# Six plain chunks instead of eight ahead of the seven-product pairs, and token-side sums made in two sets of banks

## The chip, the cores and the metric

The kernel runs on one NeuronCore of a Trainium2 chip. The metric is the device time of one execution in microseconds (us), as the median of several runs. The engines are TensorE (PE, matrix products), VectorE (DVE), ScalarE (ACT), GpSimd (POOL) and SyncE (SP, which issues the loads of weights). Each takes its instructions in order, and semaphores are the only coupling between them.

## The reference, cut to what matters

Two transformer blocks on a sequence of 512 tokens of width 1024, in float32. Each ends in a feed-forward with a hidden width of 4096, which is the part that is changed:

```python
h = rms_norm(x, norm2_g[l])
f = jnp.square(jax.nn.relu(jnp.einsum('bsd,df->bsf', h, w_ff1[l])))
x = x + jnp.einsum('bsf,fd->bsd', f, w_ff2[l])
...
h = rmsnorm(x, g_pre_mlp[layer])
u = jax.nn.relu(jnp.einsum('bsd,df->bsf', h, w_up[layer]))
y = jnp.einsum('bsf,fd->bsd', u * u, w_down[layer])
```

## The kernel before

Float32 accuracy is had from three products of rounded parts: each operand is split into a high part (`xh`, `wh`, `uh`) and a low rest (`xl`, `wl`, `ul`), and `three` issues high by high, high by low and low by high. Weights come as a stream of "chunks" of 128x1024 through four slots (chunk n in slot n % 4). SP loads `raw`, POOL rounds it to `wh` and subtracts for `wl`, and `split_ready` counts the chunks split.

Each feed-forward is done in two halves of 16 hidden tiles: an up run that makes 16 tiles of `uh` and `ul`, then a down run of 16 chunks that reads them. There are two feed-forwards, so four up runs (0 to 3). An up tile is made in one of two ways:

- A plain chunk: 24 matmuls of 512 columns (all tokens). The first three plain chunks of a run are interleaved (`several`), the others follow alone (`chunk_transposed`). PE writes chunk c to bank c % 4; the tile is evacuated with a relu, squared by ACT, and its rest is taken by DVE (`rest_of_tile`, called `rest(c)`).
- A pair: two chunks by the two halves of the tokens (EARLY, LATE), as a 2x2 product with seven products instead of eight. Each product is 12 matmuls of 256 columns. Products 1, 2 and 6 use `xh` and `xl`; products 3, 4, 5 and 7 use token-side sums (`t_high`, `t_low`), which are made once per feed-forward; products 3 to 6 use weight-side sums, which DVE makes in banks 6 and 7 for each pair (`weight_sums_first`, `weight_sums_last`), ACT rounds (`sum_round`) and DVE subtracts from (`weight_rest`). DVE also adds the seven products together (`first_corner` to `fourth_product`).

Runs 0 and 2 (the first of each feed-forward) have 8 plain chunks (`PLAIN`) and 4 pairs; runs 1 and 3 have 8 pairs. The plain chunks keep PE at work while the token-side sums are made. These come in four steps k, one for each two of the eight tiles of x: ACT writes two scaled parts (`scaled_parts`), DVE forms four sums of 256 columns over them (`t_sums` part 0), ACT rounds them (`t_round`), and DVE takes the rests (`t_sums` part 1, counted by `t_ready`). All steps use banks 4 and 5, so that step k+1 can't begin before step k is finished.

The norm's sum of squares (`norm_sums`, four transposes of `ss` into bank 7) stands in PE's queue behind the first three matmuls of plain chunk 5; `norm_total` of DVE reduces bank 7.

The order on each engine is the order of the code. For DVE it is `plain_run` and `pair_run`, for ACT `plain_tiles` and `pair_tiles`, for PE `feed_first`, `pair` and `feed_forward`, for POOL `split_rounds`, `split_chunk` and `split_pairs`.

Of the kernel before, what the change touches and what calls it, by code (L numbers as in the profile page):

```python
# [27 lines left out]
F32 = mybir.dt.float32  # L28
# [4 lines left out]
P = 128  # L33
# [30 lines left out]
PLAIN = 8  # L64
# [97 lines left out]
for _name, _n in (("norm1", 8), ("norm2", 8), ("final", 8), ("pre_mix", 8), ("post_mix", 8),  # L162
# [11 lines left out]
             (C_FF2 + 2 * FH, 3 * FH, FH // 2))  # L174
ROW_ORDER = ((0, 1, 2, 3), (1, 2, 3, 0))
# [28 lines left out]
def slot_of(p, role):  # L204

    return (PAIR_RUNS[run_of(p)][0] + role) % SLOTS
# [12 lines left out]
def build(nc, a):  # L219
    ctx = ExitStack()  # L220
    with ctx:
# [13 lines left out]
        def sem(name):  # L235
# [90 lines left out]
        t_high = [at(f"t_high{i}", [P, 4, Q], F32R, o) for i, o in  # L326
                  enumerate((behind, behind + 8192, tmb_at, tmp_at))]
        t_low = [at(f"t_low{i}", [P, 4, Q], F32R, o + 4096) for i, o in
                 enumerate((behind, behind + 8192, tmb_at, tmp_at))]
# [25 lines left out]
        x4_bank = [bank[4], bank[5], bank[6]]  # L355

# [77 lines left out]
        def product_bank(p, i):  # L434
            return bank[(7 * place_in(p) + i + run_of(p) // 3) % 5][:, EARLY]
# [109 lines left out]
        def _(pool):  # L545
# [137 lines left out]
            def split_pair(p):  # L683
# [41 lines left out]
            split_rounds(C_FF1 // SLOTS, (C_FF1 + PLAIN) // SLOTS)  # L725
            split_pairs(0)
# [11 lines left out]
            second_round = (C_FF2 + 3) // SLOTS  # L738
            for n in range(second_round * SLOTS, second_round * SLOTS + SLOTS):
                split_chunk(n)  # L740
                if n == C_FF2 + 3:
                    x4_squares()

            for n in range(second_round * SLOTS + SLOTS, C_FF2 + PLAIN):
                split_chunk(n)
# [15 lines left out]
        def _(pe):  # L761
# [334 lines left out]

            def feed_first(c0, e0, xl0, i, squares, between=None):
# [19 lines left out]
            def pair(p):  # L1117
# [8 lines left out]
                if alone:  # L1126
                    pe.wait_ge(evacuated, e - 3)
# [6 lines left out]
                if alone:  # L1134
                    pe.wait_ge(evacuated, e - 2)
# [8 lines left out]
                if alone and run in (0, 2):  # L1144
                    pe.wait_ge(t_ready, 32 if run else 16)
# [334 lines left out]
        def _(act):  # L1480
# [179 lines left out]
            def scaled_parts(k, gain):  # L1660

                if k:
                    act.wait_ge(t_ready, 4 * k - 2)
                A(bank[4][:, EARLY], x[:, k % 4, EARLY], ACT.Copy, scale=col(gain, k % 4)).then_inc(scaled_part, 1)
                act.wait_ge(t_ready, 4 * k)
                A(bank[5][:, EARLY], x[:, 4 + k % 4, LATE], ACT.Copy, scale=col(gain, 4 + k % 4)
                  ).then_inc(scaled_part, 1)

            def t_round(k):

                act.wait_ge(t_made, 4 * k + 4)
                for t, src in enumerate((bank[4][:, EARLY], bank[4][:, LATE], bank[5][:, EARLY], bank[5][:, LATE])):
                    A(t_high[t][:, k % 4], src, ACT.Copy).then_inc(t_rounded, 1)

            def sum_round(p, i):
# [3 lines left out]
                if place_in(p) == 0:  # L1679
                    act.wait_ge(chunk_done, chunk_of(p) - 3 + role)  # L1680
# [26 lines left out]
            def plain_tiles(c0, first, norm, k0, p, gain):  # L1707

                for c in range(PLAIN):
                    if c < 4:  # L1710
                        t_round(k0 + c)
# [7 lines left out]
                    if c < 3:  # L1719
                        scaled_parts(k0 + c + 1, gain)  # L1720
                    if c == PLAIN - 3:
                        norm_sd(norm)
                        sum_round(p, 0)
                        sum_round(p, 1)
                    if c == PLAIN - 2:
                        sum_round(p, 2)
                        sum_round(p, 3)
# [16 lines left out]
            act.wait_ge(xl_ready, KT + 6)  # L1744
            scaled_parts(0, "norm2")
# [204 lines left out]
            scaled_parts(4, "pre_mlp")  # L1950
# [1061 lines left out]
```

## Time and profile before

| | |
|---|---|
| median of 3 runs | 1085.52 us (1083.82 to 1086.12) |
| the profiled execution | 1085.29 us, of which the span from first to last instruction is 1083.6 us |
| PE busy | 1066.3 us, 98% of the span |
| DVE, POOL, ACT busy | 703.4, 672.5, 400.6 us |
| mean granted PE clock | 0.998 |

Busy shares are averages over the whole span. In the two changed stretches (about 158 to 230 us and 766 to 834 us) the engines have other shares: in 163.3 to 185.5 us DVE is busy for 20.08 of 22.20 us. A row of the timeline gives the start, the duration, the engine and the line, then what is written and read, and in brackets the engine's idle time ahead of it.

### The profile page before, as it was taken

To read this page: it belongs to the slowest core of one execution; us is meant where nothing else is said; L and a number is where in the kernel's file an instruction comes from. 1 tells how busy PE (TensorE), PEld (TensorE's weight loads), DVE (VectorE), ACT (ScalarE), POOL (GpSimd) and SP (SyncE) were. 2 spreads that over 40 slices of the span, in tenths; PEclk is the share of its full clock that TensorE was granted. 3 is DMA by queue.
4 is the path that set the end of the run, shared out by engine and by line. 5 is a ranking of instruction groups with operands and counts; after the bars stand their busy time and mean duration, and the time that the engine had idled before them with its cause. 6 is when DMAs were issued, how large, how long until landed. Compare 5 with 4: busy or idle time off the path is not lost.

```text
span 1083.6 us, 17261 instructions
## 1 busy us (share of the span) xinstructions
PE 1066.3 (98%) x6163; PEld 933.5 (86%) x6163; DVE 703.4 (65%) x1381; ACT 400.6 (37%) x817; POOL 672.5 (62%) x460
## 2 busy tenths in 40 slices
PE   9999999999999999999999999999999999999997
PEld 6878888998899988888788787677899888999886
DVE  5999778951158853447689878676888113886033
ACT  5156565540015541220211346655765000465012
POOL 7979856577645586667566333135856764557762
PEclk9999999999999999999999999999999999999999
DMA  7421223243223343334443232112123931234412
GB/s 261 137 96 60 69 88 98 87 147 117 97 65 111 117 156 103 110 97 138 128 123 97 79 90 67 40 53 85 59 97 124 204 102 61 96 118 168 182 59 77
DMA packets 52251, 115.54 MB, mean 107 GB/s; under 512 B 21840, under 2 KB 22480, under 8 KB 52176
## 3 DMA queue, kind: packets, MB, share of 16 engines
q1 hardware_dynamic: 31200, 105.40, 29.4%
q10 hardware_dynamic: 20976, 9.15, 3.4%
q8 instruction: 46, 0.75, 0.3%
q14 instruction: 29, 0.24, 0.1%
HBM read 105.09 MB, written 4.19 MB: 101 GB/s over the span
## 4 chain that ended last, share of the span: by engine, by line
PE 73%; DVE 18%; ACT 3%; issue 2%; POOL 2%; ACTq 1%; DMA 0%; SPq 0%; DVEq 0%; POOLq 0%
PE bank L766 71%; DVE bank L2118 5%; DVE work L2620 2%; DVE max L2613 2%; ACTq L1780 1%; DVE tmp L2010 1%; PE bank L1296 1%; POOL wl L567 1%; DVE work L2598 1%; DVE ropey L2568 1%; ACT wh L1683 1%; DMA x<-xT 0%; DVE wl L2377 0%; DVE ropey L2574 0%; DVE bank L2010 0%
## 5 line engine op out<-in xcount | busy, mean ns | idle before, releaser
L567 POOL TENSOR_TENSOR wl<-raw,wh 128x1024 fp32r<-128x1024 f32 x140 | 333.7, 2384 | 11.7
L564 POOL TENSOR_SCALAR wh<-raw 128x1024 fp32r<-128x1024 f32 x139 | 148.9, 1071 | 236.1 <-PE bank L766 181.6
L766 PE MATMUL bank<-xh,wh 128*128 128x512 f32 (+2 forms) x747 | 257.5, 345 | 2.7 <-ACT vg L1577 1.5
L766 PE MATMUL bank<-xh,wl 128*128 128x512 f32 (+2 forms) x747 | 249.1, 337 | 0.0
L766 PE MATMUL bank<-xl,wh 128*128 128x512 f32 (+2 forms) x744 | 246.9, 339 | 0.2 <-DVE xl L2029 0.2
L766 PEld LDWEIGHTS bank<-xh,wh 128*128 128x128 f32 x747 | 142.4, 191 | 33.6 <-issue 19.5
L766 PEld LDWEIGHTS bank<-xl,wh 128*128 128x128 f32 x744 | 141.4, 191 | 13.7 <-DVE xl L2029 3.1
L766 PEld LDWEIGHTS bank<-xh,wl 128*128 128x128 f32 x747 | 142.6, 191 | 11.3
L1683 ACT ACTIVATE wh<-bank 128x512 fp32r<-128x512 f32 x96 | 52.2, 596 | 241.8 <-DVE bank L2362 103.1
L766 PE MATMUL bank<-uh,wh 128*128 128x512 f32 x320 | 123.2, 385 | 1.8 <-DVE ss L2412 0.9
L766 PE MATMUL bank<-uh,wl 128*128 128x512 f32 x320 | 121.3, 379 | 0.0
L766 PE MATMUL bank<-ul,wh 128*128 128x512 f32 x320 | 117.4, 379 | 0.0
L766 PE MATMUL bank<-t_high,wh 128*128 128x256 f32 x384 | 107.1, 279 | 0.3 <-DVE sq L2418 0.2
L766 PE MATMUL bank<-t_high,wl 128*128 128x256 f32 x384 | 105.6, 275 | 0.0
L766 PE MATMUL bank<-t_low,wh 128*128 128x256 f32 x384 | 105.6, 275 | 0.0
L766 PE MATMUL bank<-wh,uh 128*128 128x512 f32 x256 | 97.1, 379 | 0.4 <-POOL wl L567 0.4
L766 PE MATMUL bank<-wh,ul 128*128 128x512 f32 x256 | 97.1, 379 | 0.0
L766 PE MATMUL bank<-wl,uh 128*128 128x512 f32 x256 | 97.0, 379 | 0.0
L2377 DVE TENSOR_TENSOR wl<-bank,wh 128x512 fp32r<-128x512 f32 x96 | 63.3, 683 | 24.3 <-ACT wh L1683 24.0
L2010 DVE TENSOR_TENSOR bank<-bank,rb 128x512 f32<-128x512 f32 x16 | 11.2, 699 | 100.8 <-PE bank L766 100.8
L701 POOL TENSOR_SCALAR wh<-raw 128x512 fp32r<-128x512 f32 x24 | 14.9, 620 | 98.9 <-PE bank L766 98.9
L766 PEld LDWEIGHTS bank<-t_high,wh 128*128 128x128 f32 x384 | 73.6, 192 | 1.6 <-issue 0.6
(338 smaller groups left out, 2108.0 us busy)
## 6 DMA issues: line engine op xcount, KB each, us to landing
raw<-wstream SPq DMA_DIRECT2D x188, 512.0 KB, 3.5
x<-xT SPq DMA_DIRECT2D x8, 256.0 KB, 4.6
x4rows<-x_rows ACTq DMA_DIRECT2D x4, 512.0 KB, 7.2
out<-x4rows SPq DMA_DIRECT2D x8, 256.0 KB, 2.1
qd<-ropey ACTq DMA_DIRECT2D x16, 64.0 KB, 2.1
kd<-ropey ACTq DMA_DIRECT2D x16, 64.0 KB, 2.4
qa<-ropey SPq DMA_DIRECT2D x16, 64.0 KB, 2.1
ka<-ropey SPq DMA_DIRECT2D x16, 64.0 KB, 2.0
```

The lines of the kernel that those rows point to most:

```text
L564: nc.gpsimd.tensor_scalar(wh[c][:], raw[c][:], 1.0, 1.0, ALU.mult, ALU.mult).then_inc(high_ready, 1)
L567: nc.gpsimd.tensor_tensor(wl[c][:], raw[c][:], wh[c][:].bitcast(F32), ALU.subtract).then_inc(split_ready, 1)
L701: nc.gpsimd.tensor_scalar(high_b[:, 0:512], b[:, 512:], 1.0, 1.0, ALU.mult, ALU.mult).then_inc(high_ready, 1)
L766: return nc.tensor.matmul(out, stationary, moved, start=start, stop=stop)
L1296: last = nc.tensor.transpose(out[:, j * P:j * P + P], probs[2 * (n % 3) + e][:, j * P:j * P + P], ident[:])
L1683: A(wh[slot_of(p, role)][:, 512 * part:512 * part + 512], bank[7 - made % 2][:], ACT.Copy).then_inc(sum_rounded, 1)
L1780: act.dma_start(dst[p0:p0 + 32, 2 * m + hh // 2, cs], ropey[32 * hh:32 * hh + 32, g % 2, part, cs]).then_inc(rope_moved[g % 2], 16)
L2010: return V.tensor_tensor(out, p, q, ALU.mult)
L2118: ins = V.scalar_tensor_tensor(out=out, in0=src, scalar=w, in1=acc, op0=ALU.mult, op1=ALU.add)
L2377: V.tensor_tensor(wl[slot][:, at], bank[7 - made % 2][:], wh[slot][:, at].bitcast(F32), ALU.subtract).then_inc(sum_ready, 1)
L2613: V.max(max8[:, q], work[:, q + 1, 0:N]).then_inc(top_step, 1)
L2620: V.match_replace(work[:, q + 1, 0:N], max8[:, q], work[:, q + 1, 0:N], TAKEN).then_inc(top_step, 1)
```

## The change

`PLAIN` goes from 8 to 6, so runs 0 and 2 have 6 plain chunks and 5 pairs. With fewer plain chunks the rest of the stage is rearranged:

- The token-side sums of steps 1 and 3 use banks 6 and 7 (`t_banks`), those of 0 and 2 banks 4 and 5. High and low parts of all four sums lie in two tensors `t_sides`, so that ACT rounds a whole bank (512 columns) in one instruction and DVE takes the rest of a whole bank in one: two instead of four each per step.
- Bank 7 is also where the norm's squares are transposed to. So PE waits in `feed_norm`, ahead of the norm's transposes, until all four steps are finished (`t_ready` 8 or 16).
- ACT waits for all eight low parts of x and for the sum of squares before the first scaled parts, since banks 6 and 7 are in use until then.
- The four slots shift by two: the weight sums of the first pair go to slots 0 to 3 as the last plain chunks leave them (`free_at`). Product 1 of the first pair goes to bank 3 and product 2 to bank 4 (`FIRST_BANK`).
- DVE and ACT have a new written order. ACT now does the tile of the last plain chunk ahead of the rounding of the first pair's weight sums.
- Four operations of a few elements each (`row_scale` to `row_weight_mean`) move from the front of `pair_run(2)` to behind it.

```diff
-PLAIN = 8
+PLAIN = 6
+FIRST_BANK = (3, 0, 3, 1)
 def slot_of(p, role):
-    return (PAIR_RUNS[run_of(p)][0] + role) % SLOTS
+    first, _, count = PAIR_RUNS[run_of(p)]
+    return (first + 2 * count + role) % SLOTS
+def free_at(p, role):
+    first = PAIR_RUNS[run_of(p)][0]
+    return first - SLOTS + (slot_of(p, role) - first) % SLOTS + 1
...
+        t_banks = [(bank[4], bank[5]), (bank[6], bank[7])]
...
+            def feed_norm(i, squares):
+                pe.wait_ge(t_ready, 16 if i == 13 else 8)
+                norm_sums(i, ss, 0, sq_added, squares)
...
-                    hooks = {0: lambda: norm_sums(i, ss, 0, sq_added, squares)} if c == 5 else {}
+                    hooks = {0: lambda: feed_norm(i, squares)} if c == PLAIN - 1 else {}
...
             def t_round(k):
                 act.wait_ge(t_made, 4 * k + 4)
-                for t, src in enumerate((bank[4][:, EARLY], bank[4][:, LATE], bank[5][:, EARLY], bank[5][:, LATE])):
-                    A(t_high[t][:, k % 4], src, ACT.Copy).then_inc(t_rounded, 1)
+                for sides, b in zip(t_sides, t_banks[k % 2]):
+                    A(sides[:, :, 0, k % 4], two(b[:]), ACT.Copy).then_inc(t_rounded, 1)
...
             def sum_round(p, i):
-                    act.wait_ge(chunk_done, chunk_of(p) - 3 + role)
+                    act.wait_ge(chunk_done, free_at(p, role))
...
-            act.wait_ge(xl_ready, KT + 6)
-            scaled_parts(0, "norm2")
+            act.wait_ge(xl_ready, 2 * KT)
+            act.wait_ge(sq_added, 2 * KT)
...
-                t_rest(0, t1, 2)
-                t_rest(1, t2, 2)
-                t_rest(2, t3, 4)
-                t_rest(3, t4, 4)
+                t_rest(0)
+                t_rest(1)
```

DVE, the beginning of run 0: behind the norm's last sum (written to `ss`) and up to the second plain tile. `L2326`/`L2345` are the sums of part 0, `L2331`/`L2351` the rests of part 1, `L2436`/`L2456` the evacuation of a tile, `L2422`/`L2440` its rest. Before:

```order
L2326 SCALAR_TENSOR_TENSOR bank4<-x_49,cols_72,bank4 128x256 [waits scaled_part]
...
L2326 SCALAR_TENSOR_TENSOR bank5<-x_49,cols_72,bank4 128x256 [waits t_made]
L2436 TENSOR_SCALAR sq0_75<-bank0 128x512 [waits chunk_done,sq_added]
L2331 TENSOR_TENSOR t_low0_143<-bank4,t_high0_139 128x256 [waits t_rounded]
...
L2331 TENSOR_TENSOR t_low3_146<-bank5,t_high3_142 128x256 [waits t_rounded]
L2422 TENSOR_TENSOR ul_65<-sq0_75,uh_64 128x512 [waits square_ready]
```

and in the changed kernel:

```order
L2345 SCALAR_TENSOR_TENSOR bank4<-x_49,cols_72,bank4 128x256 [waits scaled_part]
...
L2345 SCALAR_TENSOR_TENSOR bank6<-x_49,cols_72,bank6 128x256 [waits scaled_part]
...
L2345 SCALAR_TENSOR_TENSOR bank7<-x_49,cols_72,bank6 128x256 [waits t_made]
L2351 TENSOR_TENSOR t_sides0_139<-bank4,t_sides0_139 128x2x256 [waits t_rounded]
L2351 TENSOR_TENSOR t_sides1_140<-bank5,t_sides1_140 128x2x256 [waits t_rounded]
L2456 TENSOR_SCALAR sq0_75<-bank0 128x512 [waits chunk_done,sq_added]
L2351 TENSOR_TENSOR t_sides0_139<-bank6,t_sides0_139 128x2x256 [waits t_rounded]
L2351 TENSOR_TENSOR t_sides1_140<-bank7,t_sides1_140 128x2x256 [waits t_rounded]
```

The sums of the second step now stand ahead of the rests of the first, and up to the last rest there are three evacuations and two rests of tiles between them.

PE, plain chunk 5 of run 0, in bank 1 (`ident` by `ss` into bank 7 are the norm's transposes). Before:

```order
L766 MATMUL bank1<-xh_50,wh1_57 128x512 [waits evacuated,split_ready]
L766 MATMUL bank1<-xl_51,wh1_57 128x512
L766 MATMUL bank1<-xh_50,wl1_61 128x512
L867 MATMUL bank7<-ident_66,ss_74 128x128 [waits sq_added,bc_used]
L867 MATMUL bank7<-ident_66,ss_74 128x128 x3
```

and in the changed kernel:

```order
L772 MATMUL bank1<-xh_50,wh1_57 128x512 [waits evacuated,split_ready]
L772 MATMUL bank1<-xl_51,wh1_57 128x512
L772 MATMUL bank1<-xh_50,wl1_61 128x512
L873 MATMUL bank7<-ident_66,ss_74 128x128 [waits sq_added,bc_used,t_ready]
L873 MATMUL bank7<-ident_66,ss_74 128x128 x3
```

The place in the queue is the same, with one more wait; behind it stand the other 21 matmuls of the chunk, which is now the last plain one.

ACT, the end of the plain tiles of run 0 (`L1715`/`L1723` the relu of a tile, `L1717`, `L1718`/`L1725`, `L1726` its squares, `L1683`/`L1693` the rounding of weight sums, `L1691`/`L1701` the copy of the first product). Before:

```order
L1683 ACTIVATE wh1_57<-bank7 128x512 [waits chunk_done,sum_made]
L1683 ACTIVATE wh1_57<-bank6 128x512 [waits chunk_done,sum_made]
L1715 ACTIVATE sq0_75<-bank2 128x512 [waits ul_ready,chunk_done]
L1717 ACTIVATE uh_64<-sq0_75 128x512 [waits evacuated]
L1718 ACTIVATE sq0_75<-sq0_75 128x512
L1683 ACTIVATE wh2_58<-bank7 128x512 [waits chunk_done,sum_made]
```

and in the changed kernel:

```order
L1723 ACTIVATE sq1_76<-bank1 128x512 [waits ul_ready,chunk_done]
L1725 ACTIVATE uh_64<-sq1_76 128x512 [waits evacuated]
L1726 ACTIVATE sq1_76<-sq1_76 128x512
L1693 ACTIVATE wh1_57<-bank7 128x512 [waits chunk_done,sum_made]
L1693 ACTIVATE wh1_57<-bank6 128x512 [waits chunk_done,sum_made]
L1693 ACTIVATE wh2_58<-bank7 128x512 [waits chunk_done,sum_made]
```

The tile of bank 1 is that of the last plain chunk; it now stands ahead of all four roundings.

## Rows read from the trace of the kernel before

**Rows 1.** The page, part 1: busy time, share of the span, instructions.
```profile
span 1083.6 us, 17261 instructions
...
PE   1066.3 (98%) x6163; PEld 933.5 (86%) x6163; DVE 703.4 (65%) x1381; ACT 400.6 (37%) x817; POOL 672.5 (62%) x460
```
**Rows 2.** Waits of PE's matmuls: total us, times, longest.
```profile
PE bank L766 <- DVE soft L2671: 1.6, 1, 1.6
```
**Rows 3.** Timeline of PE, first feed-forward: start, us, instruction.
```profile
177.52 0.60 PE L867 MATMUL bank<-ident,ss 128*128 128x128 f32 x4
...
192.85 0.27 PE L766 MATMUL bank<-xh,wh 128*128 128x256 f32 x1
...
230.37 0.38 PE L766 MATMUL bank<-uh,wh 128*128 128x512 f32 x1
...
313.69 0.27 PE L766 MATMUL bank<-xh,wh 128*128 128x256 f32 x1
...
323.07 0.28 PE L766 MATMUL bank<-xh,wh 128*128 128x256 f32 x1
```
**Rows 4.** Timeline of DVE, first feed-forward.
```profile
162.72 0.68 DVE L2309 TENSOR_TENSOR ss<-sq,bank 128x512 f32<-128x512 f32 x1
...
168.28 2.22 DVE L2422 TENSOR_TENSOR ul<-sq,uh 128x512 fp32r<-128x512 f32 x1
170.43 1.78 DVE L2326 SCALAR_TENSOR_TENSOR bank<-x,cols,bank 128x256 f32<-128x256 f32 x4
172.12 0.68 DVE L2436 TENSOR_SCALAR sq<-bank 128x512 f32<-128x512 f32 x1
172.94 1.42 DVE L2331 TENSOR_TENSOR t_low<-bank,t_high 128x256 fp32r<-128x256 f32 x4
...
190.72 1.29 DVE L2377 TENSOR_TENSOR wl<-bank,wh 128x512 fp32r<-128x512 f32 x2
```
**Rows 5.** Timeline of ACT, first feed-forward.
```profile
161.92 0.46 ACT L1666 ACTIVATE bank<-x,cols 128x256 f32<-128x256 f32 x1
...
185.52 0.62 ACT L1715 ACTIVATE sq<-bank 128x512 f32<-128x512 f32 x1
...
187.22 0.58 ACT L1715 ACTIVATE sq<-bank 128x512 f32<-128x512 f32 x1
...
190.02 1.09 ACT L1683 ACTIVATE wh<-bank 128x512 fp32r<-128x512 f32 x2 [0.84 <-DVE bank L2362]
```
**Rows 6.** Timeline of POOL beside the 2.22 us row of DVE.
```profile
167.57 2.38 POOL L567 TENSOR_TENSOR wl<-raw,wh 128x1024 fp32r<-128x1024 f32 x1
169.92 1.49 POOL L564 TENSOR_SCALAR wh<-raw 128x1024 fp32r<-128x1024 f32 x1
```
**Rows 7.** Timeline of DVE, second feed-forward.
```profile
769.42 1.80 DVE L2326 SCALAR_TENSOR_TENSOR bank<-x,cols,bank 128x256 f32<-128x256 f32 x4 [2.38 <-ACT bank L1666]
...
802.95 0.42 DVE L2385 TENSOR_TENSOR sq<-bank,first_product 128x256 f32<-128x256 f32 x1
...
812.33 0.42 DVE L2385 TENSOR_TENSOR ss<-bank,first_product 128x256 f32<-128x256 f32 x1
...
822.10 0.41 DVE L2385 TENSOR_TENSOR sq<-bank,first_product 128x256 f32<-128x256 f32 x1
```
**Rows 8.** Timeline of PE, second feed-forward.
```profile
779.94 0.60 PE L867 MATMUL bank<-ident,ss 128*128 128x128 f32 x4
...
795.27 0.27 PE L766 MATMUL bank<-xh,wh 128*128 128x256 f32 x1
...
834.16 0.40 PE L766 MATMUL bank<-wh,uh 128*128 128x512 f32 x1
```
**Rows 9.** Timeline of PE behind its longest wait; busy times of 600.5 to 604 us.
```profile
599.24 1.25 PE L766 MATMUL bank<-kd,qd 64*128 64x384 f32 x4 [1.60 <-DVE soft L2671]
600.42 0.74 PE L766 MATMUL bank<-xh,wh 128*128 128x512 f32 x1
...
600.50:604.00 3.50, 3.50 (x9) 2.79 (x10) 3.46 (x9) 0.00 (x0) 0.82 (x1) 0.51 0.37 125
```

More of the change, by code:

```diff
@@ L325, in build @@
                        for r in range(len(PAIR_RUNS))]
[L326 to L329, printed above, removed]
+        t_sides = [at("t_sides0", [P, 2, 2, 4, Q], F32R, behind), at("t_sides1", [P, 2, 2, 4, Q], F32R, tmp_at)]
+        t_high = [t_sides[i // 2][:, i % 2, 0] for i in range(4)]
+        t_low = [t_sides[i // 2][:, i % 2, 1] for i in range(4)]
         work = at("work", [P, TB, S], F32, behind)
@@ L434, in product_bank @@
         def product_bank(p, i):
-            return bank[(7 * place_in(p) + i + run_of(p) // 3) % 5][:, EARLY]
+            return bank[(7 * place_in(p) + i + FIRST_BANK[run_of(p)]) % 5][:, EARLY]
         def col(name, k, n=1):
@@ L725, in _ @@
             split_rounds(C_FF1 // SLOTS, (C_FF1 + PLAIN) // SLOTS)
+            for n in range((C_FF1 + PLAIN) // SLOTS * SLOTS, C_FF1 + PLAIN):
+                split_chunk(n)
             split_pairs(0)
@@ L736, in _ @@
             split_rounds(last_round + 1, (C_FF2 + 3) // SLOTS)
-            second_round = (C_FF2 + 3) // SLOTS
-            for n in range(second_round * SLOTS, second_round * SLOTS + SLOTS):
+            for n in range((C_FF2 + 3) // SLOTS * SLOTS, C_FF2 + PLAIN):
                 split_chunk(n)
@@ L1134, in pair @@
                 if alone:
-                    pe.wait_ge(evacuated, e - 2)
+                    if run in (0, 2):
+                        pe.wait_ge(t_ready, 14 if run else 6)
                     if run == 3:
@@ L1144, in pair @@
                 if alone and run in (0, 2):
-                    pe.wait_ge(t_ready, 32 if run else 16)
+                    pe.wait_ge(t_ready, 16 if run else 8)
                 pe.wait_ge(sum_ready, 4 * p + 1)
@@ L1707, in plain_tiles, with squared @@
             def plain_tiles(c0, first, norm, k0, p, gain):
-                for c in range(PLAIN):
-                    if c < 4:
-                        t_round(k0 + c)
+                def squared(c):
                     if c >= 4:
@@ L1718, in plain_tiles @@
                     A(sq[c % 2][:], sq[c % 2][:], ACT.Square).then_inc(square_ready, 1)
[L1719 to L1727, printed above, removed]
+                scaled_parts(k0, gain)
+                scaled_parts(k0 + 1, gain)
+                t_round(k0)
+                t_round(k0 + 1)
+                scaled_parts(k0 + 2, gain)
+                squared(0)
+                scaled_parts(k0 + 3, gain)
+                t_round(k0 + 2)
+                squared(1)
+                t_round(k0 + 3)
+                squared(2)
+                squared(3)
+                squared(4)
+                norm_sd(norm)
+                squared(5)
+                sum_round(p, 0)
+                sum_round(p, 1)
+                sum_round(p, 2)
+                sum_round(p, 3)
             def pair_tiles(run):
@@ L2327, in scaled_less, with t_rest @@
                                            ).then_inc(t_made, 1)
-                def t_rest(t, src, rounded):
-                    dve.wait_ge(t_rounded, 4 * k + rounded)
-                    V.tensor_tensor(t_low[t][:, k % 4], src, t_high[t][:, k % 4].bitcast(F32), ALU.subtract
-                                    ).then_inc(t_ready, 1)
+                def t_rest(i):
+                    dve.wait_ge(t_rounded, 2 * k + i + 1)
+                    sides = t_sides[i]
+                    V.tensor_tensor(sides[:, :, 1, k % 4], two(t_banks[k % 2][i][:]),
+                                    sides[:, :, 0, k % 4].bitcast(F32), ALU.subtract).then_inc(t_ready, 1)
                 if part == 0:
```

58 lines of the change are left out of this document (31 added, 27 removed).

## The prediction

> **What bounds the kernel now.** I read the page first, then the waits of PE, then the timelines of PE, DVE, ACT and POOL over the two changed stretches. PE is busy for 1066.3 of 1083.6 us [rows 1], and its longest wait for another engine in the whole span is 1.6 us [rows 2]: whatever is taken from PE's own stream is gained, and whatever it is made to wait for is lost. The other engines matter only where one of them is late for PE.
>
> What a plain chunk and a pair cost PE is read from starts. From 230.37 to 313.69 us PE does 16 plain chunks of the down run and four transposes (about 0.4 us): 82.9 / 16 = 5.18 us a chunk [rows 3]. From 313.69 to 323.07 it does one pair: 9.38 us, or 1.34 us a product [rows 3]. Run 0's four pairs take 230.37 - 192.85 = 37.52 us, exactly four times 9.38: PE never waits there. Run 2's four take 834.16 - 795.27 = 38.89 us [rows 8], 1.37 us more. The reason is DVE: it starts `first_corner` of successive pairs at 802.95, 812.33 and 822.10 us, so up to 9.77 us apart [rows 7], which is longer than PE's 9.38, and at the first of them it is 802.95 - (795.27 + 2.68) = 5.0 us behind the product that it adds. So a lag of some 5 us is all that PE can hide, and beyond that a pair costs 9.77 instead of 9.38 us.
>
> **The matmuls.** Twice, two plain chunks (10.36 us) become one pair (9.38 us): -0.98 us each, **-1.96** in all. Had nothing else to be paid, 1083.3 us would follow.
>
> **The wait ahead of the norm's transposes.** PE comes to them at 177.52 us in run 0 [rows 3], and nothing ahead of that place in its queue is changed. Before, they waited for squares that were long there; now they wait for all rests of the token-side sums, and 21 matmuls of the chunk and every pair are queued behind them. When is DVE done? The norm's last sum ends at 162.72 + 0.68 = 163.40 us [rows 4]. ACT now begins only then, and two scaled parts at some 0.4 us apart, the second 0.46 long [rows 5], bring DVE's first sum to 164.4. From there DVE has, up to the last rest:
>
> - 4 steps of four sums, each step 172.12 - 170.43 = 1.69 us [rows 4]: 6.76.
> - 8 rests of 512 columns in two rows of 256. No such row exists. Four rests of 256 columns take 1.42 us, 0.36 each [rows 4]: the bounds are one of them (0.36, twice the columns at no more time) and two (0.71, nothing saved). `L2377` has 512 columns and reads a bank and a rounded tensor in the same way: two in 1.29, which is 0.61 start to start beside the tail [rows 4]. I take that, the same kind and size: 4.88 (2.9 to 5.7 by the bounds).
> - 3 evacuations of 0.68, 0.60 start to start: 1.80 [rows 4].
> - 2 rests of tiles, 0.61 each undisturbed: 1.22.
>
> That is 14.66 us, and 0.1 for the last one's end: 179.15 us with no idle time at all. Before, this same work had until 192.85 + 2.68 = 195.5 us (product 3). Idle time comes on top. A rest of a tile can stretch: the row at 168.28 lasted 2.22 us because it stood still until POOL's `L567` ended at 167.57 + 2.38 = 169.95, and POOL's next, at 169.92, was held in turn (1.49 us) [rows 4, 6]. Each of the two rests can so cost 0 to 1.6 us. I take 0.85 for both and for the waits on ACT: 180.0 us, a wait of **2.5 us** in run 0 (bounds 1.6 and 4.9, or 0.5 with rests of 0.36).
>
> The Trainium skill, SBUF — State Buffer, section "SBUF: two separate sides", has the rule behind the stretched row: DVE and GpSimd share a pair of ports under an exclusive lock, which a VectorE operation with two SBUF inputs needs and whoever comes first keeps for the whole instruction. By that rule the new rests, which read a bank, are never held; if they were, as the two tile rests are, eight holds of up to 1.6 us would come on top. The stretched and held rows agree with it, and `L2377` rows show no stretch.
>
> In run 2 the sums start at 769.42 us [rows 7] and PE comes at 779.94 [rows 8]: only 10.5 us for the same 14.76, which gives 784.2. With 0.3 of idle time, 784.5: a wait of **4.6 us** (bounds 4.2 and 7.4, or 2.6 with rests of 0.36). A part of it falls earlier, since the evacuation of chunk 0 now stands behind four steps' worth of DVE work and chunk 4 needs its bank.
>
> **The first pair.** Its weight sums go into slot 1, which the last plain chunk holds, and ACT does that chunk's tile first. From the end of the chunk (its last matmul's result is there some 0.15 us after PE moves on): relu and two squares 187.22 - 185.52 = 1.70 [rows 5], rounding 0.60 (two in 1.09), DVE's rest 0.68 [rows 4], and 0.15 for three handovers: 3.3 us. Product 3 needs it after 2.68: a wait of 0.6. Then DVE has two weight sums, a tile rest, a reciprocal and another rest, ACT a rounding between, again about 3.2 to 3.3 us from the first rest to the third, which product 5 needs 2.68 us behind product 3: 0.5. With a matmul's slow restart after each wait, **1.2 us** (bounds 0.6, and 2.8 if that tile rest is held by POOL once).
>
> **The following pairs.** DVE then starts `first_corner` some 5 us behind PE, just the lag that run 2 had at its start [rows 7]. What followed there is what follows now in both runs, with one pair more: the pairs from the third on cost 9.77 instead of 9.38, **0.9 us** in each run (bounds 0.4 and 1.6). In run 2 the 1.37 us that were lost before are replaced by these: -1.37. The four small operations moved behind run 2 free DVE of about 1.8 us ahead of `first_corner`, and the lag above is reckoned without them.
>
> **The sum at full clock.** Run 0: -0.98 + 2.5 + 1.2 + 0.9 = +3.6. Run 2: -0.98 + 4.6 + 1.2 + 0.9 - 1.37 = +4.35. Together +8.0 us. Runs 1 and 3, both down runs and the attention are not touched; PE is as full there as before and gives nothing back.
>
> **PE's clock.** Behind its 1.60 us wait and four small matmuls the granted clock of 600.5 to 604.0 us is 0.51, so the lower level of 1.2 GHz, and nine matmuls take that stretch, where the chunks above (5.18 / 24 = 0.216 us a matmul) would have 16 in it [rows 9]: about 1.6 us lost. PE's new waits, 2.5 and 4.6 us, are longer than that, so a fall behind the second is likely and behind the first an even chance. A fall costs 1.6 us, but DVE goes on meanwhile and its lag shrinks, so that about 0.5 comes back: +1.1 each. One fall is the likeliest: **+9.1 us** on 1085.29, 1094.4. The profiled execution lies 0.23 us below the median of the runs shown, so this is 1094.6 for the median; I round towards the case without a fall and say **1094.2**.
>
> The Trainium skill, TensorE: Matmul & The Clock Gate, section "Why this matters for your kernels", advises against idle gaps between bursts of matmuls because TensorE's clock falls back to half. By it the second wait here, the longest of the kernel, is at risk and the first less so; without any such fall the sum would be the +8.0 above.
>
> **Rivals.**
> - *The sums are in time* (the other side). If DVE reached its last rest by 177.5 and 780 us, only -1.96 and up to -1.37 of run 2's old loss would remain: 1082.2 to 1083.6. It needs DVE to do 14.66 us of back-to-back work in 13.1 and 10.5 us; the point from which it decides is a rest of 512 columns at under 0.41 us for run 0 and under 0.1 us for run 2, so only run 0 could get there, and run 2 would then still wait 2.6 with rests of 0.36. For it speaks only that the rests' shape is new. Chance 0.05.
> - *Only the norm's wait is real*: ACT's order and DVE's lag are hidden. Then -1.96 + 2.5 + 4.6 - 1.37 = +3.8, 1089.3. For it: run 0 had no loss in its pairs before. Against: its DVE lag at the start was smaller, and the chain from the last chunk to product 3 is longer than 2.68 us by rows. Chance 0.08.
> - *The clock never falls*: +8.0, 1093.5. Against it stands only one row, that of 1.60 us; chance 0.27.
> - *One fall or two* (forecast): +9.1 to +10.2, 1094.6 to 1095.7. Chance 0.48.
> - *Worse*: POOL holds the tile rests ahead of both waits and in the first pairs, +3 more: 1097 to 1099. Each hold exists in rows; several together are rare. Chance 0.10.
> - *The wait moves PE into DVE's time and the two cancel*, no change within 0.2% (about what a measurement of this kernel can tell from none): 0.02.
>
> **How the numbers follow.** Faster 0.05, same 0.02, slower 0.93. The range reaches from between the second rival and the sum at full clock to the beginning of the worst case: 1090.5 to 1097.0 leaves out about 2 in 10.
>
> **What the changed profile should show.** A wait of PE for DVE ahead of the transposes of `ss` (`L873`), 2 to 3 us near 180 and 4 to 5 us near 784; DVE without idle time in the 15 us ahead of each; `t_sides` rests of about 0.61 us start to start; two waits of about half a microsecond at the third and fifth product of the first pair, for DVE's `wl`; five pairs in 48.5 to 49.5 us instead of 46.9; a stretch with a granted clock near 0.5 behind the second wait. The prediction is wrong if the transposes start at 177.5, or if the pairs of run 0 take 46.9 us.

## The result and the profile after

The changed kernel takes 1097.04 us in the median of four executions (1095.14, 1095.27, 1098.81, 1102.96), the kernel before 1084.67 (1083.72 to 1086.12); the ratio is 1.0124, with a 95% interval of 1.0107 to 1.0141. The sign and the mechanisms are as forecast, but the median lies above the range that ended at 1097.0. The execution in the trace is the fastest one, 1095.14 us (forecast for it: 1094.4). Most of what a longer execution has more lies outside the feed-forwards; run e1 shows it.

The page of the changed kernel, part 1 (answers to [rows 1]), and then those waits of PE's matmuls that are new or stood at the top before (total, times, longest; answers to [rows 2]):

```profile
span 1093.4 us, 17399 instructions
...
PE   1066.1 (98%) x6235; PEld 933.9 (85%) x6235; DVE 710.7 (65%) x1395; ACT 405.2 (37%) x811; POOL 667.3 (61%) x462
```
```profile
PE bank L873 <- DVE t_sides L2351: 6.1, 2, 3.7
PE bank L772 <- issue: 1.7, 3, 0.9
PE bank L772 <- DVE wl L2395: 1.7, 2, 1.3
PE bank L772 <- DVE tmp L2082: 1.5, 1, 1.5
PE bank L772 <- DVE soft L2697: 1.5, 1, 1.5
```

PE is busy as long as before and the span is 9.8 us longer: the loss is in waits. The first and the third row are new, and so is most of the second. Their places are in the timeline of PE (start, duration, and in brackets the idle time ahead):

```profile
180.74 0.66 PE L873 MATMUL bank<-ident,ss 128*128 128x128 f32 x4 [2.35 <-DVE t_sides L2351]
...
185.77 0.27 PE L772 MATMUL bank<-xh,wh 128*128 128x256 f32 x1
...
196.56 0.28 PE L772 MATMUL bank<-xh,wh 128*128 128x256 f32 x1
...
224.71 0.28 PE L772 MATMUL bank<-xh,wh 128*128 128x256 f32 x1
...
234.48 0.38 PE L772 MATMUL bank<-uh,wh 128*128 128x512 f32 x1
...
777.69 0.45 PE L772 MATMUL bank<-xh,wh 128*128 128x512 f32 x1 [0.57 <-DVE sq L2456]
...
787.47 1.11 PE L873 MATMUL bank<-ident,ss 128*128 128x128 f32 x4 [3.71 <-DVE t_sides L2351]
...
794.08 0.27 PE L772 MATMUL bank<-xh,wh 128*128 128x256 f32 x1
...
797.79 0.46 PE L772 MATMUL bank<-t_sides,wh 128*128 128x256 f32 x2 [0.87 <-issue]
...
806.11 0.28 PE L772 MATMUL bank<-xh,wh 128*128 128x256 f32 x1
...
834.26 0.29 PE L772 MATMUL bank<-xh,wh 128*128 128x256 f32 x1
...
844.04 0.38 PE L772 MATMUL bank<-wh,uh 128*128 128x512 f32 x1
```

Both waits for the token-side sums stand ahead of the transposes, and chunk 4 of run 2 waits too (777.69), as the forecast said. The first pairs take 196.56 - 185.77 = 10.79 and 806.11 - 794.08 = 12.03 us instead of 9.38, the next three in either run (224.71 - 196.56) / 3 = 9.38, the last ones 9.77 and 9.78.

DVE ahead of and in the first pair of run 2, and POOL beside it:

```profile
797.00 1.29 DVE L2395 TENSOR_TENSOR wl<-bank,wh 128x512 fp32r<-128x512 f32 x2 [5.76 <-ACT wh L1693]
...
799.53 1.74 DVE L2440 TENSOR_TENSOR ul<-sq,uh 128x512 fp32r<-128x512 f32 x1
```
```profile
799.45 1.27 POOL L705 TENSOR_TENSOR wl<-raw,wh 128x512 fp32r<-128x512 f32 x1
```

DVE idles 5.76 us there: for the first three the slot is still held by the last plain chunk, which PE ends at 794.08, and then ACT does that chunk's tile (1.7 us) ahead of the rounding. And a tile's rest stands still until POOL's operation ends at 800.72. That hold is most of why run 2's first pair costs 1.2 us more than run 0's: the rest takes 1.74 us, the same one in run 0 takes 0.86.

The granted clock (the eighth value) of 4 us behind either wait, and of 3.5 us at the place of [rows 9]:

```profile
180.70:184.70 4.00, 3.96 (x21) 3.53 (x22) 3.96 (x5) 1.64 (x4) 1.14 (x1) 1.00 0.01 4
787.50:791.50 4.00, 4.00 (x14) 3.44 (x15) 3.69 (x6) 2.83 (x6) 0.00 (x0) 0.60 0.00 0
```
```profile
604.60:608.10 3.50, 3.50 (x18) 2.58 (x17) 3.50 (x7) 0.33 (x3) 1.33 (x1) 1.00 0.28 68
```

Of the two waits only the second is followed by the lower level of the clock. Behind the wait of 1.5 us near 604 it stays up here, though the kernel before fell there. By the starts of its matmuls the changed kernel gets 1.7 us back at this place (from 600.42 to 604.80 it took 4.38 us, from 604.95 to 607.64 it takes 2.69). Some 0.4 of it had been lost ahead, at a wait of 0.17 us in the attention, so that the stretch between the feed-forwards is 1.3 us shorter in all.

### The profile page after: what moved, and what is told of

Read it like the earlier page. It is cut to its first block, busy times and chain, and to the rows that moved or that the text cites. A ratio compares the mean times of both kernels' runs of the same rounds, so it can differ in the third digit from the quotient of the medians.

```text
span 1093.4 us, 17399 instructions
## 1 busy us (share of the span) xinstructions
PE 1066.1 (98%) x6235; PEld 933.9 (85%) x6235; DVE 710.7 (65%) x1395; ACT 405.2 (37%) x811; POOL 667.3 (61%) x462
## 4 chain that ended last, share of the span: by engine, by line
PE 70%; DVE 20%; issue 3%; ACT 3%; POOL 2%; ACTq 1%; DMA 1%; SPq 0%; DVEq 0%; POOLq 0%
PE bank L772 69%; DVE bank L2136 5%; DVE work L2646 2%; DVE max L2639 2%; ACTq L1799 1%; DVE bank L2345 1%; DVE tmp L2028 1%; PE bank L1308 1%; DVE t_sides L2351 1%; POOL wl L575 1%; DVE bank L2028 1%; DVE work L2624 1%; DVE xl L2047 1%; DMA x<-xT 1%; DVE ul L2440 0%
## 5 line engine op out<-in xcount | busy, mean ns | idle before, releaser
L575 POOL TENSOR_TENSOR wl<-raw,wh 128x1024 fp32r<-128x1024 f32 x136 | 323.8, 2381 | 11.3
L572 POOL TENSOR_SCALAR wh<-raw 128x1024 fp32r<-128x1024 f32 x135 | 144.0, 1067 | 235.1 <-PE bank L772 178.2
L772 PE MATMUL bank<-xh,wh 128*128 128x512 f32 (+2 forms) x739 | 251.8, 341 | 3.0 <-ACT vg L1589 1.5
L772 PE MATMUL bank<-xh,wl 128*128 128x512 f32 (+2 forms) x739 | 243.2, 333 | 0.0
L772 PE MATMUL bank<-xl,wh 128*128 128x512 f32 (+2 forms) x736 | 241.0, 335 | 1.1 <-DVE xl L2047 1.0
L1693 ACT ACTIVATE wh<-bank 128x512 fp32r<-128x512 f32 x104 | 56.5, 595 | 249.4 <-DVE bank L2380 100.5
L772 PE MATMUL bank<-t_sides,wh 128*128 128x256 f32 x832 | 144.7, 277 | 3.1 <-DVE wl L2395 1.7
L772 PEld LDWEIGHTS bank<-t_sides,wh 128*128 128x128 f32 x832 | 126.1, 192 | 5.0 <-DVE wl L2395 2.1
L772 PE MATMUL bank<-t_sides,wl 128*128 128x256 f32 x416 | 114.4, 275 | 0.0
L2395 DVE TENSOR_TENSOR wl<-bank,wh 128x512 fp32r<-128x512 f32 x104 | 68.5, 682 | 33.1 <-ACT wh L1693 33.1
L772 PEld LDWEIGHTS bank<-t_sides,wl 128*128 128x128 f32 x416 | 79.9, 192 | 0.0
```

What stands on the lines that cost most here:

```text
L572: nc.gpsimd.tensor_scalar(wh[c][:], raw[c][:], 1.0, 1.0, ALU.mult, ALU.mult).then_inc(high_ready, 1)
L575: nc.gpsimd.tensor_tensor(wl[c][:], raw[c][:], wh[c][:].bitcast(F32), ALU.subtract).then_inc(split_ready, 1)
L772: return nc.tensor.matmul(out, stationary, moved, start=start, stop=stop)
L1693: A(wh[slot_of(p, role)][:, 512 * part:512 * part + 512], bank[7 - made % 2][:], ACT.Copy).then_inc(sum_rounded, 1)
L2395: V.tensor_tensor(wl[slot][:, at], bank[7 - made % 2][:], wh[slot][:, at].bitcast(F32), ALU.subtract).then_inc(sum_ready, 1)
```

## The experiments

Each is timed beside the kernel before on the same chip; its median there was 1083.97 to 1084.3 us. "Undisturbed" means the executions of a kernel's lowest level (in e2 and e11 a single one). e2 to e4, e6, e7, e9 to e14 are edits of the changed kernel, e5 and e8 of the kernel before.

**e1: the changed kernel again.**

> The changed kernel once more, to see how its executions spread. The one in the trace took 1095.14 us, others 1095.27, 1098.81 and 1102.96 at a mean clock of 0.997, 0.996 and 0.993. Theory 'spread by the new waits': the times again lie between 1095 and 1103 while those of the kernel before stay within 3 us of each other; the longer ones have a lower mean clock; a profile over 1096 us shows a stretch near half clock at a place where the trace of 1095.14 us has full clock, behind one of the new waits (run 0's transposes or the first pairs). Rival 'spread of the chip': the kernel before spreads as widely in the same rounds, or all executions of the changed one lie within 1094.5 to 1096.

Six executions: 1096.54, 1096.66, 1103.7, 1104.61, 1104.83, 1105.1; those of the kernel before, eleven, lie within 1083.54 to 1086.82. The execution in the trace is that of 1105.1. PE's longest wait in 500 to 580 us (the only other one there is 0.6), and the matmul that waited:

```profile
PE bank L772 <- DVE tmb L2028: 5.4, 1, 5.4
```
```profile
564.64 0.80 PE L772 MATMUL bank<-wh,xh 128*128 128x512 f32 x1 [5.36 <-DVE tmb L2028]
```

That is in the attention, at the index scores, 330 us behind the changed code. Followed back from there: DVE in this stage is held by POOL time and again (the row at 551.58 lasts 2.60 us, in the first trace 0.48).

```profile
551.58 2.60 DVE L2621 TENSOR_SCALAR work<-sq,wnat 128x512 f32<-128x512 f32 x1
...
557.42 3.80 DVE L2624 SCALAR_TENSOR_TENSOR work<-sq,wnat,work 128x512 f32<-128x512 f32 x2 [0.68 <-ACT sq L1819]
```
```profile
551.20 2.69 POOL L575 TENSOR_TENSOR wl<-raw,wh 128x1024 fp32r<-128x1024 f32 x1
...
558.02 2.67 POOL L575 TENSOR_TENSOR wl<-raw,wh 128x1024 fp32r<-128x1024 f32 x1
```

The first of these holds, two rows of DVE and the two of POOL beside them:

```profile
527.49 1.34 DVE L2624 SCALAR_TENSOR_TENSOR work<-tmp,wnat,work 128x256 f32<-128x256 f32 x1
528.87 2.35 DVE L2629 TENSOR_TENSOR work<-work,mask 128x128 f32<-128x128 f32 x1
```
```profile
527.52 1.04 POOL L572 TENSOR_SCALAR wh<-raw 128x1024 fp32r<-128x1024 f32 x1 [2.90 <-PE bank L772]
528.64 2.42 POOL L575 TENSOR_TENSOR wl<-raw,wh 128x1024 fp32r<-128x1024 f32 x1
```

In the first trace the row of 1.34 us lasts 0.49 (525.51) and is nearly over when POOL starts (525.96), and the one behind it lasts 1.11. DVE meets POOL here because it is 0.4 us late from 525 us on, and it is late because ACT is. ACT issues eight rope transfers (`qd<-ropey`) ahead of its copies of the scores. This group in the kernel before, and here:

```profile
513.43 5.01 ACTq L1780 DMA_DIRECT2D qd<-ropey  x8
```
```profile
519.16 6.04 ACTq L1799 DMA_DIRECT2D qd<-ropey  x8
```

Seven issues last at most 0.61 us and one, at 522.91, lasts 1.65. In 523.0 to 523.2 us the DMA view names a packet of another kind:

```profile
q8 instruction: 1, 0.02, 35.4%
```

So a transfer of 16 KB of instructions passes just there. In the trace of the kernel before such packets stand in 501.2 to 501.3, 524.7 to 524.8 and 553.8 to 553.9 us. Only the first meets issues, those of the group ahead (one of which is 1.26 us long), and no wait of PE follows. In the changed kernel's first trace they stand in 521.5 to 521.6 and 547.7 to 547.8. PE itself is 4.1 us later there (234.48 against 230.37), so in its program they have moved forward by 7 and 10 us: it has 72 matmuls more in the two feed-forwards, half of them ahead of this place, and so more instructions. That execution, of 1095.14 us, had a lengthened issue too (eight in 5.61 us) and came through with a wait of 0.2. The clock falls behind the wait of 5.4 us (0.50 in 564.6 to 568.6 us) and behind the transposes at 180 us (0.57), which it didn't in the first trace. Of the 9.9 us between the two traces 6.9 arise between the two feed-forwards, 1.7 are the fall of the clock at 180 us, and 1.4 a longer fall behind the second wait (803.99 - 795.97 = 8.02 us from the transposes to the first pair, 6.61 in the first trace). Theory "spread by the new waits" has this one part right, the clock.

**e2: the norm's transposes later.** In `feed_first`:

```diff
-hooks = {0: lambda: feed_norm(i, squares)} if c == PLAIN - 1 else {}
+hooks = {6: lambda: feed_norm(i, squares)} if c == PLAIN - 1 else {}
```

> The norm's wait and transposes stand behind 21 matmuls of the last plain chunk instead of 3 (in both feed-forwards). Theory 'place': the waits of 2.5 and 3.7 us and the clock's fall of 1.6 us are paid because 21 matmuls stand behind them; they go and nothing comes for them: about 1087.5 us against 1095.1. Rival 'backlog of DVE': norm_total, and with it weight_sums_first in the same bank 7, now comes later on DVE, and the wait reappears at product 3 of the first pair for wl, some 2 to 3 us longer than it was there; only the clock's fall is saved: 1093 to 1094 us.

Undisturbed 1093.97 us (median 1099.49, ratio 1.0125, 1.0104 to 1.0146). No wait for `t_sides` is left, but one at product 3 of each first pair:

```profile
189.66 0.76 PE L772 MATMUL bank<-t_sides,wh 128*128 128x256 f32 x2 [3.79 <-issue]
```

It was 0.52 there. "Backlog of DVE" is right: 2.35 us are removed, and 3.3 us come back. Behind both waits the clock falls. The execution in the trace (1098.97 us) has a wait of 3.1 us at the index scores too.

**e3: ACT rounds first.** In `plain_tiles`, `squared(5)` stands behind `sum_round(p, 1)`:

```diff
-squared(5)
 sum_round(p, 0)
 sum_round(p, 1)
+squared(5)
```

> ACT rounds the first pair's two first weight sums ahead of the tile of the last plain chunk (relu and two squares, 1.7 us), in both feed-forwards; nothing else is changed. Theory 'order on ACT': the first pair's excess (1.4 us in run 0, 2.65 in run 2 over 9.38) is ACT's tile in front of the rounding; it goes, and 1091 to 1091.5 us result. Rival 'DVE is full anyway': the pairs' work is DVE's 9.77 us a pair, so later pairs take 9.77 instead of 9.38 and give most of it back: 1093.5 to 1094.5 us. Both waits ahead of the transposes stay at 2.5 and 3.7 us.

Undisturbed 1092.86 us (median 1094.45, ratio 1.0099, 1.0077 to 1.0121). No wait is left in the first pairs, but the five pairs take 48.43 us in either run instead of 48.71 and 49.96: all of them cost 9.45 to 9.8, none 9.38. "DVE is full anyway" is the nearer theory; only where POOL's hold was avoided, in run 2, 1.5 us are gained.

**e4: both edits.**

> The norm's transposes behind 21 matmuls, and ACT's two roundings ahead of the last plain tile, together. Theory 'backlog of DVE': in the former alone the wait at product 3 was 3.95 us, of which ACT's tile of 1.7 us is a part, so 1.4 to 1.7 us of each go: 1090.5 to 1091.5 us for the undisturbed executions (1093.97 and 1092.86 for either alone). Rival 'sum of both': -1.2 and -2.3 add up, 1091.6. Rival 'nothing more': 1092.5 or above.

Executions of 1088.7, 1088.82, 1090.93, 1090.99, 1094.1 and 1094.2 us; median 1090.96, ratio 1.0064 (1.0047 to 1.0081). The lowest level is some 2 us below all three expectations: with the waits cut to 1.5 and 1.2 us in run 0 and 1.9 and 0.6 in run 2, PE's clock doesn't fall in either feed-forward (mean 0.998).

**e6: matmuls in the wait.** In `feed_norm`, whose results in bank 4 nothing uses:

```diff
+pe.wait_ge(t_ready, 14 if i == 13 else 6)
+for k in range(WARM):  # 12
+    mm(bank[4][:], wh[...][:, 0:P], xh[:, k % 8], start=True, stop=True)
 pe.wait_ge(t_ready, 16 if i == 13 else 8)
```

> Twelve extra matmuls of 512 columns (their result in bank 4 is not used) run between t_ready 6 (14) and t_ready 8 (16), that is inside the norm's wait, 2.6 us of work at 0.216 us each. Theory 'clock': the waits for DVE stay, but the granted clock behind the second one stays at 1.0, the 1.6 us of it are saved (less what DVE's lag takes back), 1093.5 to 1094.5 us in the median, and the executions of 1098 and 1103 us are gone. Rival 'no effect': t_ready 6 comes too late or the matmuls delay the transposes by some of their 2.6 us: 1095 us or more.

Undisturbed 1093.23 us, 1.9 below 1095.14; median 1094.53, ratio 1.0099 (1.0079 to 1.0118). The clock behind both waits is 1.00: 1.6 us of the second wait's cost is the clock. The executions of 1099 us remain; the one in the trace has the attention's 5.4 us.

**e5: the kernel before, with the small operations moved behind `pair_run(2)`** (the last hunk of the change alone).

> The kernel before, with nothing but the four small operations of the row scale moved behind run 2's pairs. Theory 'DVE's lag': they take about 1.8 us ahead of first_corner; DVE starts the pairs that much earlier and the 1.37 us that run 2 lost shrink to 0 to 0.4: 1082.7 to 1083.2 us against 1084.0. Rival 'no effect': POOL and ACT set those holds, 1083.8 to 1084.2.

Median 1083.24 us (1082.68 to 1084.98), ratio 0.9990 (0.9982 to 0.9999). Run 2's pairs take 833.38 - 795.47 = 37.91 us instead of 38.89: 0.98 of the 1.37 us are back. "DVE's lag" is right.

**e7, e8: where the instructions' transfers fall.** Waits that have long been met, spread over PE's products of run 1 (`PADS` places with the pair of waits below; the expectations count one extra instruction for each):

```diff
 for k in range(4):
+    if done[0] < PADS and run_of(pairs[0]) == 1 and k in (1, 2, 3):
+        pe.wait_ge(split_ready, 1)
+        pe.wait_ge(split_ready, 2)
+        done[0] += 1
```

> The changed kernel with 60 extra waits on semaphores that have long been reached, spread over PE's products of run 1, so that the 16 KB instruction transfers of queue q8 come about 6 us earlier in the attention's stage (near 515 and 541.5 us instead of 521.6 and 547.8) and meet none of ACT's rope transfers. Theory 'instruction transfers': ACT's issues last 0.61 us each there, PE's wait of 5.4 us near 556 us and the half clock behind it are gone in every execution: all times within 1094 to 1098 us, median 1095.5 (a fall of the clock behind the wait at 180 us may still add 1.6). Rival 'chance of the ports': the spread has nothing to do with these transfers, and half of the executions or more stay at 1103 to 1105, median near 1100.

> The kernel before with 76 such waits in the same products, so that its instruction transfers stand to the attention's stage as they do in the changed kernel (near 517.5 and 543.6 us instead of 524.8 and 553.9); its feed-forwards are not touched. Theory 'instruction transfers': it gets the wait near 552 us in a part of its executions, with 1090 to 1093 us there and 1084 to 1085 in the others, median above 1085. Rival: 1083.5 to 1087 as ever, median 1084.

e7 missed its aim: the packet came in 520.3 to 520.4 us, still beside the issues (519.2 to 525.4), and the executions are spread as before, 1094.66 to 1104.97 (median 1099.18); it tells nothing of executions that are free of the packet. e8 met its: the packet stands in 517.8 to 517.9 us, eight issues last 6.43 us, one of them 2.03, and PE waits at the index scores:

```profile
514.00 6.43 ACTq L1788 DMA_DIRECT2D qd<-ropey  x8
```
```profile
559.47 0.80 PE L767 MATMUL bank<-wh,xh 128*128 128x512 f32 x1 [5.36 <-DVE tmb L2018]
```

Four of twelve executions take 1090.78 to 1091.41 us, the others 1084.33 to 1086.3; the median is 1085.08 (ratio 1.0016, 1.0000 to 1.0033). Of the unpadded kernel before none of the 64 timed beside these runs took more than 1086.82. The feed-forwards are untouched in it.

**e9, e13: the changed kernel with 112 such waits.**

> The changed kernel with 112 instead of 60 extra waits. With 60, the transfer of queue q8 stood at 520.39 us, still inside ACT's issues of 519.2 to 525.4, so that run tested nothing; 52 more should move it by 2.5 to 5 us, ahead of the first of them. Theory 'instruction transfers': the two groups of issues last 5.0 us each, no wait of 5.4 us near 556 to 560 us in any execution, times within 1094 to 1098, median 1096. Rival: executions of 1102 to 1105 remain although no transfer meets an issue.

> The kernel with 112 extra waits once more, since it had only four executions (1094.03 to 1096.22). Theory 'instruction transfers': again none above 1098. Rival 'chance': with the rate of the unpadded kernel (about half of the executions at 1102 to 1105) some six more executions hold about three of them.

In e9 the packets stand in 511.3 to 511.4 and 535.5 to 535.6 us. The first meets the group ahead and one issue there lasts 1.65 us, without harm; the group in question is free, and so is the next:

```profile
516.95 5.01 ACTq L1807 DMA_DIRECT2D qd<-ropey  x8
```

All eight executions lie within 1094.03 and 1096.45 us, medians 1094.86 and 1095.11, ratios 1.0098 (1.0083 to 1.0112) and 1.0098 (1.0082 to 1.0113). Without the waits six of ten had lain at 1098.8 or above.

**e14: e4 with the 112 waits.**

> The late transposes and early roundings with the 112 waits. Without them the executions were 1088.7, 1088.8, 1090.9, 1091.0, 1094.1 and 1094.2. Theory 'instruction transfers': only 1088 to 1091 remain (the rest is TensorE's clock), median 1089.5. Rival 'chance': the level of 1094 stays.

Five executions within 1087.99 and 1089.75 us, median 1088.26, ratio 1.0039 (1.0025 to 1.0052): both upper levels of e4 are gone.

Over all sixteen traces the picture is this. In six of them (before, e5, e9, e12, e13, e14) no packet meets the first group of eight `qd` issues, the group lasts 5.0 to 5.2 us, and PE doesn't wait at the index scores. In the other ten a packet meets it. Where it then lasts 6.04 us or more (e1, e6, e7, e8), PE waits 5.4 us. Where it lasts 5.54 to 5.99, the wait is 0.2 to 0.5 us, but 3.1 in e2 (5.95).

**e11, e10: short rests.** In the second feed-forward the eight rests of the sums have 64 instead of 512 columns, and its products read `t_high` in place of `t_low` (those low parts are left out; PE's work is the same):

```diff
+n = 32 if k >= 4 else Q
-V.tensor_tensor(sides[:, :, 1, k % 4], two(t_banks[k % 2][i][:]),
-                sides[:, :, 0, k % 4].bitcast(F32), ALU.subtract).then_inc(t_ready, 1)
+V.tensor_tensor(sides[:, :, 1, k % 4, 0:n], two(t_banks[k % 2][i][:])[:, :, 0:n],
+                sides[:, :, 0, k % 4, 0:n].bitcast(F32), ALU.subtract).then_inc(t_ready, 1)
```

> The changed kernel with the eight rests of the second feed-forward's sums shortened from 512 to 64 columns; the products of runs 2 and 3 read the high parts in place of the low ones, so PE's work is the same, and the low parts of that feed-forward's sums are left out. Each rest then takes some 0.12 instead of 0.61 us, DVE is 3.9 us earlier. Theory 'backlog of DVE, one to one': the waits of 0.73 and 3.87 us (4.6) shrink to about 0.7 together and the clock's fall behind them goes: 1095.1 - 3.9 - 1.6 = 1089.6 us for undisturbed executions. Rival 'ACT's roundings are the bound': the wait stays above 2.5 us and the time above 1092. The first feed-forward stays as it is.

> The late transposes and the early roundings (1088.7 us where undisturbed) with the same eight short rests in the second feed-forward. There 0.73, 1.88 and 0.62 us of waits and about 1.2 us of longer pairs remained in it. Theory 'backlog, one to one': the three waits go, -3.2, 1085.5 us. Rival 'the wait moves on': DVE's 9.77 us a pair bound the later pairs, which take 0.39 each and give about 1.2 us back, 1086.7.

e11, undisturbed, 1092.17 us. Of 0.57 and 3.71 us of waits, 1.42 are left:

```profile
786.00 0.66 PE L873 MATMUL bank<-ident,ss 128*128 128x128 f32 x4 [1.42 <-DVE t_sides L2353]
```

By the starts 4.6 us of waits have become 1.6: 3.0 of the some 3.8 us that DVE was given reach PE (two short rests take 0.26 us where two long ones took 1.20). The rest is new idle time of DVE, 0.17 and 0.54 us for ACT. The clock's fall of the second wait is gone as well, but the one near 604 us is back in this execution. e10, undisturbed, 1087.47 us, is 1.2 below e4: both expectations (1085.5, 1086.7) were too low. The waits of 1.1 and 1.2 us in the first pair stay. There DVE has no backlog: it idles 0.97 us for PE's transposes. But each wait has a tile's rest ahead of the weight rest that PE needs, and POOL holds it:

```profile
787.94 1.74 DVE L2442 TENSOR_TENSOR ul<-sq,uh 128x512 fp32r<-128x512 f32 x1
789.60 1.28 DVE L2397 TENSOR_TENSOR wl<-bank,wh 128x512 fp32r<-128x512 f32 x2
```
```profile
787.85 1.28 POOL L712 TENSOR_TENSOR wl<-raw,wh 128x512 fp32r<-128x512 f32 x1
```

Alone such a rest takes 0.68 us, so the hold is 1.1 of it, and 0.9 at the other (792.12, 1.62 us). In e4 the two waits of run 0 have the same holds ahead of them (184.35, 1.74 us; 188.67, 1.49 us). No run has this order without the holds.

**e12: eight plain chunks with the rest of the change** (`PLAIN = 8`, `FIRST_BANK = (0, 0, 0, 1)`, transposes in chunk 6, two tiles more as before).

> The changed kernel with eight plain chunks again (the first count alone undone; the norm's transposes stand late in chunk 6, the two tiles more go as in the kernel before): two sets of banks, rounding of whole banks and the moved small operations remain. Theory 'too little cover': with 10.36 us more of PE's work ahead of the pairs every wait is gone, 1082.5 to 1083.5 us, as in the kernel before with the moved operations (1082.68 to 1083.2). Rival 'the new sums are slow themselves': waits ahead of the transposes or in the first pair remain, 1085 us or more.

Median 1083.2 us (1082.88 to 1085.24), ratio 0.9991 (0.9982 to 1.0). No wait is left ahead of the transposes or in the pairs (one of 0.6 us at chunk 4 of run 2 is): "too little cover" is right, and the new sums are not slow themselves. They are not faster either: e5, which lacks them, takes 1083.24. These two are the only versions below the kernel before, by about 1 us.

## Why the prediction was wrong, point by point

**The matmuls**: right. Pairs two to four take 9.38 us, PE's waits apart the exchange is worth -0.98 in each run.

**The wait ahead of the transposes**: right to 0.1 us. Forecast 2.5 and 4.6; measured 2.51 in run 0 by the starts, and 0.73 + 3.87 = 4.60 in run 2. A rest of 512 columns takes 0.60 from start to start:

```profile
168.50 1.28 DVE L2351 TENSOR_TENSOR t_sides<-bank,t_sides 128x512 fp32r<-128x512 f32 x2
169.70 0.68 DVE L2456 TENSOR_SCALAR sq<-bank 128x512 f32<-128x512 f32 x1
```

e2 and e11 show that the wait is DVE's backlog: it moves with the place, and shrinks with DVE's work.

**The first pair**: the mechanism right, one size off. 1.41 us in run 0 (forecast 1.2), 2.65 in run 2, where the hold that was kept for the upper bound (2.8) took place.

**The following pairs**: 0.39 us in each run instead of 0.9. DVE does take 9.77 us a pair, as forecast:

```profile
193.51 0.41 DVE L2403 TENSOR_TENSOR sq<-bank,first_product 128x256 f32<-128x256 f32 x1
202.87 0.41 DVE L2403 TENSOR_TENSOR ss<-bank,first_product 128x256 f32<-128x256 f32 x1
212.64 0.41 DVE L2403 TENSOR_TENSOR sq<-bank,first_product 128x256 f32<-128x256 f32 x1
```

Reckoned as in the forecast, its lag in the first pair is 193.51 - (185.77 + 2.68) = 5.1 us, the 5 us that were forecast. But the first pair's own waits hold PE and not DVE, and take the lag down to 202.87 - (196.56 + 2.68) = 3.6; it then grows by 0.39 a pair and reaches 4.8 in the last one alone, which costs 9.77. In run 2 of the kernel before and in e3, pairs behind the first cost 9.76 to 9.79 where the lag is 4.8, and 9.45 where it is 4.5. The forecast counted both the first pair's waits and the full lag behind them.

**The clock**: one fall, behind the second wait, as taken. It costs 794.08 - 787.47 = 6.61 against 5.03 us, 1.6; of it the forecast gave 0.5 back for DVE's lag, and no row shows that. e1 has both falls, and its second costs 3.0 us.

**The sum.** Run 0: -0.98 + 2.51 + 1.41 + 0.39 = +3.3; run 2: -0.98 + 4.60 + 2.65 + 0.40 - 1.37 + 1.58 = +6.9. That is +10.2 against a forecast of +9.1. The first 100 us were 0.8 longer, and the stretch between the feed-forwards 1.3 shorter: +9.7, of the 9.8 by which the spans differ. So the 0.7 us between forecast and execution are in part luck: the first pairs (+1.7) and the clock (+0.5) cost more than forecast, the following pairs less (-1.0), and the last two terms were not in the forecast.

**The step that failed** is in "the sum at full clock": "Runs 1 and 3, both down runs and the attention are not touched". It put everything outside the two stretches at nothing. Not one instruction of the attention's order is changed, and PE is as full there, but the change made PE's program longer ahead of it, and the transfers that bring the instructions moved against ACT's issues. The traces of e1, e6 and e7 show what this costs: a wait of 5.4 us and a fall of the clock. That the other long executions have the same, or a part of it, is inferred from their times (in e1 1103.7 to 1105.1 against 1096.6 us, and 1098.81 and 1102.96 among the first four, which carry the median over the range). With the transfers moved away (e9, e13) the changed kernel takes 1094.9 and 1095.1 us, inside the range and within 1 us of the number. The same step stands behind the 0.23 us by which the forecast goes from one execution to the median: it took for granted that the changed kernel's executions agree among themselves as closely as those of before.

**The rivals**: "the sums are in time" and "only the norm's wait is real" are refuted by the rows; "worse" had the right size for the wrong reason. The Trainium skill, SBUF — State Buffer, section "SBUF: two separate sides", says that where a VectorE operation that needs the shared ports meets one of GpSimd, the one which starts first keeps them for the whole instruction. The rows agree where POOL is first (799.45 and 799.53; 551.20 and 551.58); at 527.49 and 527.52 the two start together, and DVE is the one held. The new rests, which read a bank, show no hold in run 0 (four rows of two, 1.27 to 1.28 us each; POOL's 168.24 to 170.62 lies beside the first).

Open is why one lengthened issue leads to the wait of 5.4 us in some executions and to 0.2 in others (1095.14 us had 5.61 us of issues, e1 6.04): the traces differ by 0.4 us in ACT's end, and DVE meets POOL's operation at 527.52 or just misses it, but no experiment changed this alone, and e2 and e3 (5.95 us with a wait of 3.1, 5.99 with 0.3) show that the length of the issues doesn't decide it by itself.

## What to carry to other kernels

Cover is counted in the time of the slowest helper: two chunks fewer of PE's work ahead of a stage saved 1 us and took away 10.4 us of time in which DVE made its operands. A wait that is moved to a later place comes back there if the engine behind it is full, so find the backlog first and shorten that. And a change in the number of instructions moves the transfers of the program behind it: where the times of a changed kernel spread more than before, compare its traces far away from the change too, and pad the stream by a few waits to see whether the spread goes.

## What the runs showed of the hardware

- Semaphores are not all that couples the engines. A tile's rest of DVE takes 0.68 us alone and 1.74 beside POOL's operation (799.53 us in the changed kernel, 787.94 in e10), and the transfers of PE's instructions reach ACT's issues.
- Instructions come in packets of 16 KB (queue q8, kind instruction, 0.9 to 1.6 us each). That they are PE's follows from this, that waits added to PE alone moved them: 76 pairs of waits moved one by 6.9 us (524.7 to 517.8). The shift is not in proportion: measured from the start of ACT's group, 60 pairs gave 2.8 us (e7 against e1) and 112 gave 9.5 (e9 against the first trace).
- An issue of a DMA by ACT that meets such a packet lasts 1.2 to 2.0 us instead of 0.61 (at 501.35 us in the kernel before 1.26, 522.0 in the changed one 1.21, 522.9 in e1 1.65, 517.8 in e8 2.03, 520.4 in e7 1.30). Not every long issue has one: e7's at 523.03 lasts 1.06 with no packet beside it.
- Behind the same wait of 2.5 us at 180 us the clock fell in four traces (e1, e3, e7, e13; 0.57 in e1) and stayed up in three (the first, e9, e11; 1.00). Behind the wait of 3.7 us it fell in all six traces that have it (the first, e1, e3, e7, e9, e13), at a cost of 1.4 us (e9) to 3.0 us (e1). Behind the 1.5 us near 604 it fell in the kernel before and in e11, and not in the first trace of the changed kernel.
